# Layer 1's feed-forward in two phases, with its down projection as one seven-product block multiplication

## The reference

```
def swiglu(a, wg, wu, wd):
    return (jax.nn.silu(a @ wg) * (a @ wu)) @ wd
```

## Time and profile before

| | |
|---|---|
| median of three runs | 3269.39 us |
| span of the profiled execution | 3271.7 us |
| TensorE busy in the span | 3100.0 us (95%) |
| GpSimd busy | 1887.5 us (58%) |
| VectorE busy | 1864.1 us (57%) |
| ScalarE busy | 1003.9 us (31%) |
| mean granted TensorE clock | 0.979 |
| first matmul of layer 1's seven-product part | 2632.28 us |
| last matmul begins | 3268.03 us |

### The profile page before, as it was taken

How to read it: one execution, slowest core, us unless ns; L and a number is a source line. 1 busy time by engine, 2 the same in 40 slices (tenths; PEclk the granted TensorE clock), 3 DMA queues, 4 the chain that set the end, 5 groups by cost and what they waited for, 6 DMA issues and landing times. The chain is left out here.

```text
span 3271.7 us, 43749 instructions
## 1 busy us (share of the span) xinstructions
PE 3100.0 (95%) x14814; PEld 2549.7 (78%) x14814; DVE 1864.1 (57%) x2502; ACT 1003.9 (31%) x1761; POOL 1887.5 (58%) x1700
## 2 busy tenths in 40 slices
PE   7998998999999999999898979999998999999999
PEld 6777876788888888888786757777776778888887
DVE  5585665555444444444535557777766765454454
ACT  4323675140000000000333447676672311010110
POOL 3584775652222222222433258888888688888884
PEclk9999998999999999999999989999999999999999
DMA  6367223322122121211122441111114111111112
GB/s 234 111 201 202 69 57 120 123 71 67 63 64 64 64 64 58 63 59 59 51 80 98 144 137 40 47 40 39 47 29 146 61 45 58 45 51 58 52 47 81
DMA packets 123537, 262.52 MB, mean 80 GB/s; under 512 B 35184, under 2 KB 66160, under 8 KB 123312
## 3 DMA queue, kind: packets, MB, share of 16 engines
q1 hardware_dynamic: 110256, 217.76, 21.2%
q10 hardware_dynamic: 13184, 43.52, 4.4%
HBM read 217.60 MB, written 43.58 MB: 80 GB/s over the span
## 5 line engine op out<-in xcount | busy, mean ns | idle before, releaser
L1546 POOL TENSOR_TENSOR a_pl<-a_p,a_ph 128x512 fp32r<-128x512 f32 x320 | 450.7, 1430 | 103.4 <-ACT a_p L1491 98.4
L2483 DVE SCALAR_TENSOR_TENSOR residual<-ps,mod,residual 128x512 f32<-128x512 f32 (+1 forms) x440 | 302.8, 696 | 312.0 <-PE ps L164 312.0
L128 POOL TENSOR_TENSOR small<-ident 128x1 f32<-128x1 f32 x108 | 41.6, 385 | 704.0 <-PE ps L164 407.3
L164 PE MATMUL ps<-mixed_hi,l_whi 128*128 128x512 f32 (+1 forms) x1200 | 426.4, 355 | 6.0 <-PE ps L164 4.0
L164 PE MATMUL ps<-mixed_lo,l_whi 128*128 128x512 f32 (+1 forms) x1200 | 425.5, 355 | 0.0
L164 PE MATMUL ps<-mixed_hi,l_wlo 128*128 128x512 f32 (+1 forms) x1200 | 425.2, 354 | 0.0
L164 PE MATMUL ps<-hidden,l_whi 128*128 128x512 f32 (+1 forms) x1056 | 284.2, 357 | 6.3 <-POOL l_wlo L139 5.1
L164 PE MATMUL ps<-a_q,a_k 97*128 97x512 f32 x960 | 273.2, 398 | 1.2 <-POOL a_q L1565 1.2
L164 PEld LDWEIGHTS ps<-mixed_hi,l_whi 128*128 128x128 f32 x1200 | 227.3, 189 | 40.0 <-issue 8.1
L164 PEld LDWEIGHTS ps<-mixed_lo,l_whi 128*128 128x128 f32 x1200 | 227.4, 189 | 31.5
L164 PEld LDWEIGHTS ps<-mixed_hi,l_wlo 128*128 128x128 f32 x1200 | 227.1, 189 | 31.7
(11 more groups left out here) (355 smaller groups left out, 7413.6 us busy)
## 6 DMA issues: line engine op xcount, KB each, us to landing
l_raw<-in_w_ffn SPq DMA_DIRECT2D x66, 512.0 KB, 3.6
raw<-in_w_ffn SPq DMA_DIRECT2D x66, 512.0 KB, 3.7
l_vraw<-in_mod_t ACTq DMA_DIRECT2D x48, 512.0 KB, 3.7
f_vraw<-in_mod_t ACTq DMA_DIRECT2D x24, 512.0 KB, 4.1
a_k<-scratch_k SPq DMA_DIRECT2D x32, 320.0 KB, 7.0
f_raw<-in_w_in SPq DMA_DIRECT2D x16, 512.0 KB, 5.2
l_raw<-in_w_out SPq DMA_DIRECT2D x16, 512.0 KB, 3.8
raw<-in_w_out SPq DMA_DIRECT2D x16, 512.0 KB, 4.5
```

Source lines behind the costliest of these rows:

```text
L128: e.nc.gpsimd.tensor_tensor(e.spare[:, 0:1], e.ident[:, 0:1], e.ident[:, 0:1], ALU.mult)
L164: last = nc.tensor.matmul(out, a, b, start=at == 0, stop=at == n - 1)
L1546: nc.gpsimd.tensor_tensor(pl[:, kk % 2, c], p[:, kk % 2, c], ph[:, kk % 2, c].bitcast(F32), ALU.subtract).then_inc(s["pl"], 1)
L2483: last = nc.vector.scalar_tensor_tensor(h[:, m, a:a + w], e.ps[:, o:o + w], e.mod[:, g, c:c + 1], h[:, m, a:a + w], ALU.mult, ALU.add)
```

## The change

Layer 1 gets a function of its own, `mixer_ffn1`; `mixer_ffn` stays for layer 0. Up to the first pair of hidden tiles the lists are as before. Then:

**Phase one** is a loop of 10 pairs with gate and up only: 14 products of 12 matmuls, in the order 1, 2, 7, 6, 5, 4, 3, with seven PSUM banks. The high of each weight half is made by ScalarE, the low and the sums by GpSimd; the instructions that settle are gone. There are seven slots for halves and four raw blocks. The gated pair is not split: VectorE makes its four block sums (`hidden_factors`), and SyncE stores the seven blocks (128 x 3584, 1.84 MB) to DRAM.

**Phase two** is down as one 2 x 2 block multiplication over the whole hidden width, in seven products of 11 steps; a step is 4 output tiles x 3 = 12 matmuls, with four PSUM banks that are summed over the 11 steps. For each step a hidden piece (128 x 512) is loaded from DRAM and split by ScalarE and VectorE, ring of six; the 44 quarter blocks of down weights are all loaded into the room of the activations that phase one no longer needs. VectorE makes the sums of these weights (`down_combine`) in place. 56 evictions (`evict`) add the products to the residual.

The diff, cut to what the lists do:

```diff
+GATE_ORDER = (1, 2, 7, 6, 5, 4, 3)
+DOWN_ORDER = (1, 2, 4, 7, 6, 5, 3)
+DOWN_INTO = {1: ((0, 0), (0, 1), (1, 0), (1, 1)), 2: ((0, 0),), 4: ((1, 0),), 7: ((1, 0), (1, 1)), 6: ((0, 1), (1, 0), (1, 1)),
+             5: ((0, 1), (1, 1)), 3: ((0, 1),)}
+BRING, BRAW = 6, 8
...
+            @block.sync
...
+                store_hidden(0)
+                with each(sp, LASTI) as i:
+                    load_mid(i + 1, 1, i * HALVES + 6)
+                    load_mid(i + 1, 0, i * HALVES + 7)
+                    store_hidden(i + 1)
+                    load_mid(i + 1, 3, i * HALVES + 13)
+                    load_mid(i + 1, 2, i * HALVES + 14)
+                sp.wait_ge(s["half"], mid.iters * HALVES)
+                sp.wait_ge(s["hstored"], 16 * (pairs - 1))
+                for st in range(4):
+                    load_hidden(st)
+                for k in range(8):
+                    load_down("11", k)
+                for st in range(4, BRAW):
+                    load_hidden(st)
+                for k in range(8, pairs):
+                    load_down("11", k)
+                store_hidden(pairs - 1)
+                for st in range(BRAW, steps):
+                    load_hidden(st)
...
+                def store_hidden(pair):
+                    sp.wait_ge(s["tprod"], pair * 4 + 4)
...
+            @block.gpsimd
...
+                def half(i, pos, of):
+                    pool.wait_ge(s["half_hi"], i * HALVES + pos + 1)
+                    nc.gpsimd.tensor_tensor(half_slot(pos, 1), of, half_slot(pos, 0).bitcast(F32), ALU.subtract).then_inc(s["half"], 1)
...
+                def matrix(i, j, p0, x0, between=None):
+                    half(i, p0, a11)
+                    combine(i, x0, a11, a11, a21, ALU.subtract)
+                    half(i, p0 + 1, a12)
+                    half(i, p0 + 2, a11)
+                    combine(i, x0 + 1, a11, a22, a11, ALU.subtract)
+                    if between:
+                        between()
+                    half(i, p0 + 3, a11)
+                    combine(i, x0 + 2, a12, a12, a11, ALU.subtract)
+                    combine(i, x0 + 3, a21, a21, a22, ALU.add)
+                    half(i, p0 + 4, a21)
+                    half(i, p0 + 5, a22)
+                    half(i, p0 + 6, a12)
...
+            @block.tensor
...
+                def down_step(st):
+                    pe.wait_ge(s["alo"], st + 1)
+                    pe.wait_ge(s["blo"], st + 1)
...
+                    if k == pairs - 1:
+                        pe.wait_ge(s["bank"], P * 4 + 4)
+                        pe.sem_inc(s["step"], 1)
...
+            @block.scalar
...
+                def gate_part(i):
+                    gate_copy(i)
+                    for x in range(7):
+                        weight_high(i, 7 + x)
+                        if x in (2, 6):
+                            for z in ((0,) if x == 2 else (1, 2, 3)):
+                                act.wait_ge(s["gadd"], i * 7 + (1, 5, 6, 7)[z])
+                                q = quarter[((0, 0), (1, 0), (1, 1), (0, 1))[z]]
+                                nc.scalar.activation(q, q, ACT.Silu).then_inc(s["gsilu"], 1)
...
+                with each(act, LASTI) as i:
+                    gate_part(i)
+                    up_copy(i)
+                    for x in range(7):
+                        weight_high(i + 1, x)
+                gate_part(LASTI)
+                up_copy(LASTI)
+                for st in range(steps):
+                    down_high(st)
+                    hidden_high(st)
...
+            @block.vector
...
+                    add(1, 1, b11, b12)
+                    gated_product(i, 0)
+                    add(2, 3, b12, b12)
+                    add(3, 2, b22, b12)
+                    add(4, 4, b12, b12)
...
+                    add(5, 5, b21, b22)
+                    gated_product(i, 1)
+                    add(6, 4, b22, b22)
+                    gated_product(i, 2)
...
+                    add(7, 6, b12, b12)
+                    gated_product(i, 3)
+                    hidden_factors(i + 1, i * 4 + 8)
...
-            mixer_ffn(e, "l1", stream, h, hi, lo, LAT, dram["w_out1"], dram["w_ffn"][1], 1,
-                      (gated[:, 0, :], gated[:, 1, :], hid[:, 0:2, :], hid[:, 2:4, :]), out=out, mixp=mixp, split=RING)
+            mixer_ffn1(e, stream, h, hi, lo, acts_at, dram["w_out1"], dram["w_ffn"][1], (gated[:, 0, :], gated[:, 1, :]), hid, out, mixp)
```

More of the change, by code:

```diff
@@ L2677, in _ @@
                 dve.wait_ge(t["ss"], 2)
+GATE_ORDER = (1, 2, 7, 6, 5, 4, 3)
+DOWN_ORDER = (1, 2, 4, 7, 6, 5, 3)
+DOWN_INTO = {1: ((0, 0), (0, 1), (1, 0), (1, 1)), 2: ((0, 0),), 4: ((1, 0),), 7: ((1, 0), (1, 1)), 6: ((0, 1), (1, 0), (1, 1)),
+             5: ((0, 1), (1, 1)), 3: ((0, 1),)}
+DOWN_PLACE = {1: "11", 2: "12", 4: "22", 7: "11", 6: "11", 5: "21", 3: "12"}
+HIDDEN_SLOT = {(0, 0): 0, (1, 0): 1, (0, 1): 5, (1, 1): 6}
+T4, T3, T2, T1 = 2, 3, 4, 5
+DOWN_GROUPS = ((0, 1), (2, 3, 4), (5, 6, 7), (8, 9, 10))
@@ L3410, in program @@
             ("q1", (HEADS1, QK1, LAT), F32), ("k1", (HEADS1, QK1, T), F32), ("sum", (1, LAT), F32),
-            ("v1", (TT, 128, HEADS1 * VD1), F32), ("h", (KT, 128, LAT), F32))}
+            ("v1", (TT, 128, HEADS1 * VD1), F32), ("h", (KT, 128, LAT), F32), ("hidden", (HT // 2, 128, 7 * BANK), F32))}
         e.ps = top.enter_context(nc.psum_tensor("ps", [128, 8 * BANK], F32))
@@ L3508, in program @@
         with ExitStack() as c:
+            acts_at = -(-nc.sbuf_base // 32) * 32
             hi, lo = acts(c, "o1", LAT)
@@ L3513, in program @@
             attention1(e, hi, lo, h, mixp, dram["w_out1"], ring_at)
-            hid, gated = e.sbuf(c)("hidden1", [128, 4, LAT], F32R), e.sbuf(c)("gated1", [128, 2, LAT], F32)
-            mixer_ffn(e, "l1", stream, h, hi, lo, LAT, dram["w_out1"], dram["w_ffn"][1], 1,
-                      (gated[:, 0, :], gated[:, 1, :], hid[:, 0:2, :], hid[:, 2:4, :]), out=out, mixp=mixp, split=RING)
+            hid, gated = e.sbuf(c)("hidden1", [128, 7, BANK], F32), e.sbuf(c)("gated1", [128, 2, LAT], F32)
+            mixer_ffn1(e, stream, h, hi, lo, acts_at, dram["w_out1"], dram["w_ffn"][1], (gated[:, 0, :], gated[:, 1, :]), hid, out, mixp)
 def _rope(rot_dim):
@@ L3570, in _lay_out @@
     for p in range(1, HT // 2):
-        paired += [("g", 2 * p), ("g", 2 * p + 1), ("h", 2 * p - 2), ("h", 2 * p - 1), ("u", 2 * p), ("u", 2 * p + 1)]
-    paired += [("h", HT - 2), ("h", HT - 1)]
+        paired += [("g", 2 * p), ("g", 2 * p + 1), ("u", 2 * p), ("u", 2 * p + 1)]
+    paired += [("h", x) for x in range(HT)]
     ffn_w = []
```

597 lines of the change are left out of this document (added).

## The result

| | before | after |
|---|---|---|
| median of the runs, us | 3269.57 (3264.27 to 3273.68, 6 runs) | 3281.68 (3278.49 to 3288.39, 6 runs) |
| span of the profiled execution, us | 3271.7 | 3280.9 |
| granted TensorE clock, mean | 0.979 | 0.977 |

The ratio is 1.0041, with a 95% interval of 1.003 to 1.0053: 12 us slower, 9.2 us by the two spans. That lies in the range of the prediction (3239 to 3290, 51 us wide), but 11.7 us above its 3270, outside the 3263 to 3276 of its likeliest case, and on the slow side of the 0.2% that was set for "no change".

What follows compares the result with a forecast made beforehand. TensorE was taken to bound the kernel before, the ring the changed loop. 29.9 us gained and 2.6 at the start, against 2.1 and about 32 given back, made 3272.6, 0.9 more; median 3270, range 3239 to 3290.

Steps and rivals of the forecast that it cites:

- likeliest case: Loop of phase one: a pass from 41.2 to 42.6 us, total 3263 to 3276 us; chance 30%.
- the ring: Phase one: up blocks land, highs, sums, silus, copy, VectorE's sums, factors, store, next landing; 42.0 us against TensorE's 38.08.
- The signs that were set for it: Loop trace: TensorE idle 2 to 4 us before first up product, clock under 1, VectorE products over 1.1, store 5 to 7.
- the work removed: TensorE: 2604 matmuls instead of 2736, 132 fewer at 0.2267 us, 29.9 us less if always fed.
- First iteration: Start of the seven-product part: 44.7 us from 2632.3, 6.6 lost instead of 9.2; first queued up blocks land at 2694.4.
- nothing at the change of phase: Between loop and down products: no net gain, 4.8 us lost for 5.4 before; first down step 25.0 after last landing.
- TensorE's own waits: Phase two: TensorE waits seven times for its own last matmul, 0.3 us each, 2.1 us together.
- Shorter pass: Loop: VectorE gets its turn before GpSimd, factors at 31.1, pass 40.3, 15 us less, 3255 us; chance 25%.
- TensorE stays the bound: Loop: pass below 38.1 us, with turns without price and shorter DMA, total 3236 us; chance 12%.
- Longer pass: Loop: eight VectorE instructions each wait a full turn, 13.5 instead of 11.0 us, pass 44.5, total 3293; chance 22%.
- VectorE bounds phase two: Phase two: turns of 1.3 us use up the 13.6 us lead, 8 to 14 us lost, total 3281; chance 11%.
- The path to memory: Store and two up blocks in the ring: 9.2 us using the trace's 402 GB/s; the skill's 358 would add 0.85 a pass.

Runs made afterwards that it cites:

- the sums over 8 columns: Changed kernel with the four sums of hidden blocks made over 8 columns instead of 512 after the first iteration (wrong result): 3247.15 us, one run.
- first experiment: Changed kernel with SyncE loading the next pair's two up blocks ahead of the store of hidden factors: 3237.73 us, 0.9908 of the kernel before.
- third experiments: Changed kernel with every hidden pair stored twice and the blocks loaded ahead of the store: 3241.75 us, one run.
- The two experiments on the order: Changed kernel with eight down pieces issued before the hidden pieces: 3273.84 us; then also hidden lows 4 and 5 ahead of the last up sum: 3273.11 us.
- the last experiment: Kernel with up blocks loaded ahead of the store, TensorE signalling a product's end after three matmuls of the next: 3233.29 us, 0.9893 of the kernel before.
- the doubled store: Changed kernel with every hidden pair stored twice, both ahead of the up blocks: 3320.75 us, one run.

## Why the prediction came out as it did

**Right: the bound and the ring.** The forecast had a ring of 42.0 us through SyncE, ScalarE, VectorE and the store, over TensorE's 38.08. Eight passes took 337.5 us, 42.19 each. Its steps, landing taken as 0: copy at 16.4 (measured 16.1), factors at 32.8 (32.7), store and up blocks 9.2 (9.4). The gated products and factors, 11.0 us by turns with GpSimd from the earlier trace rows, took 11.05 (1.63 + 1.24 + 0.98 + 1.39, 1.67 + 1.78 + 0.69 + 1.67); that turns are what they pay is shown by the sums over 8 columns. The signs that were set for it came: gated products with a mean of 1.28 us, three of the four factors with means of 1.57 to 1.78, the store landed after 6.8. Only the place of TensorE's waits was not quite as said, as some passes have a second one before the fifth up product, and the clock was under 1.00 in three of the eight. That the order and not the bytes makes the ring is shown by the first and third experiments.

**Right: the work removed.** The profiles count 14814 matmuls before and 14682 after, 132 fewer. Once fed, the kernel is 0.92% under the one before, 30 us. Counted within the traces from the first matmul of the seven-product part to the end, it takes 604.7 us instead of 639.4: 29.9 of the 34.7 are the matmuls, and most of the rest is the change of phase, where the kernel before loses 5.4 by the forecast's count and this one next to nothing.

**First iteration: mis-sized, and hidden by luck.** The forecast counted from 2632.3, where the kernel before begins this part. This execution began it at 2628.66, 3.6 us earlier; in the nine traces with the new lists it begins between 2625 and 2638. From its start the first 14 products took 46.0 us, not 44.7 (the sixth waited 2.63 us for VectorE's factors, until 20.0 after the start, forecast 17.7), and the first queued up blocks landed after 64.5, not 62.1. So the landing at 2693.1 for 2694.4, and the last landing at 3030.4 exactly as forecast, are in part luck: 2.4 us longer here, 1.3 longer in eight passes, 3.6 early.

**Wrong: "nothing at the change of phase".** Two terms failed here. From the last landing to the first down step I had 25.0; it took 27.6, as ScalarE's first down high stands ahead of everything and waits for two down pieces, which SyncE issued behind four hidden pieces; the second took 5.74 us and landed 24.9 after the last landing. I had let these six land at 22.8. And the first product was given 30.2 + 2.4 for the clock; it took 36.9: 30.2, 1.8 for the clock at its start, 3.04 idle before the fifth step, and 1.9 behind that, where the granted clock fell a second time (0.68, then 0.79 until 3080). I had walked SyncE, ScalarE and TensorE, but not VectorE's list: hidden lows 0 to 3 stand between its last up sums, wait for ScalarE's highs, and hold up the factors, and hidden low 4, that the fifth step needs, is behind those. Together 6.9 us more than forecast. The two experiments on the order took 9.0 us out by the traces, part of it the clock loss that was forecast, so the cause is shown: the order on SyncE for the start, the order on VectorE for the fifth step.

**Mis-sized: TensorE's own waits.** 0.3 each were allowed, made of 0.16 for the overlap that is lost and 0.15 of hand-over. It is 0.6: the hand-over took 0.29 to 0.30, and the next product starts more slowly. Over phase two that made 1.4 us more than forecast.

**The sum.** From the start of the seven-product part 640.3 us were forecast (2632.3 to 3272.6) and 652.2 measured (2628.66 to 3280.9). The 12 us more are 2.4 of the first iteration, 1.3 of eight passes, 6.9 of the change of phase and 1.4 of own waits. That is also the distance of the medians, 3281.7 for 3270; the forecast sum and the span are only 8.3 apart because this execution began the part early. All four misses have the same sign, and the 51 us of the range held them.

**The rivals.** *Shorter pass*: GpSimd was first, its low began at 2794.33 and the first gated product at 2794.55, which took 1.63 us; the margin was 0.2 us, so this could have fallen otherwise. *TensorE stays the bound* came only when the order was undone (3237.7 against its 3236). *Longer pass* decided from 42.6; it was 42.2, so the slow result is not that rival, though it has its sign. *VectorE bounds phase two* named 3281, the time that was measured, but that is chance: VectorE was busy 170 of 220 us, and in the last experiment TensorE ran its 924 matmuls without a stop beside the same work of VectorE, so the lead of six pieces was enough. What VectorE did hold up, the fifth step, is the order of its list at the change of phase.

**The path to memory.** With the about 358 GB/s that the Trainium skill gives (SBUF — State Buffer, section A bandwidth-pool intuition that's wrong) store and blocks would have been 10.05 us on my count, an estimate from its figure (8.05 and the ramp of 2.0); they took 9.4, the forecast with 402 was 9.2. In slices of the 40 us around 2780 the trace reads, in GB/s:

```profile
GB/s 0 0 0 0 0 0 0 0 100 358 459 459 258 201 254 397 422 414 434 176 0 0 0 0 0 0 0 0 0 0 0 0 0 0 0 0 0 0 0 0
```

It passes 400 in five slices of 1 us and falls to 201 between: the mean over the 9 us from 2768.5 is 346. That mean holds the ramp, which my count had beside the 402, and some bytes of the gate blocks that are queued behind. So the trace does not agree with 358 as a limit of the path, though the mean of such a burst comes near it.

## What to carry to other kernels

Where one engine issues stores and loads from a list in order, as SyncE here, put a store that waits for the end of an iteration behind the loads that the next one needs: here that order alone is worth some 44 us (3281.7 to 3237.7), and the bytes of a second store of 1.84 MB cost a pass nothing there. To price a change that adds such a wait, walk the ring once round from landing to landing, and compare it with the busy time of the bounding engine. At a change of phase walk the list of every engine, the idle one's too: one of the two waits here was on an engine busy 58% of the time. And compare a forecast with a trace from an event at the start of the changed part: here the position in the whole span hid 3.6 us.

## What the runs showed beyond that

- A wait of TensorE for its own last matmul costs 0.6 us, twice the idle time that the trace puts before the next matmul: 213.06 against 209.45 us for 924 matmuls and six such waits.
- A VectorE sum of two SBUF tiles over 8 columns took 0.15 and 0.17 us, or 1.14 and 1.26 where it waited for its turn with GpSimd; over 512 columns 0.69, or 1.67 and 1.78. What such a sum loses beside GpSimd is not in proportion to its size (1.0 to 1.1 us at either).
- A store of 1.84 MB ahead of two blocks of 0.52 MB delays them 4.3 us (from the doubled store), 427 GB/s, a little faster than the 402 of the earlier trace rows.
- After 4.55 us without work TensorE began the down products at a granted clock of 0.53 over the first 3.41 us, that is, near its lower level of 1.2 GHz. After the gaps of 0.3 us between products it stayed at 1.00 (first experiment, last line). After waits of nearly the same length before the first up product it differed: 0.58 over the 3.24 us from 2821.76 behind 2.34 us idle, and 1.00 over the 2.39 us from 2779.61 behind 2.48. So the length of the last wait alone does not tell what clock is granted.

```profile
3086.90:3090.00 3.10, 3.08 (x14) 2.55 (x15) 2.69 (x4) 1.06 (x2) 1.29 (x1) 1.00 0.39 126
```
